# A hybrid mixer and top-4-of-32 expert layer on one core: selection and ranks inside the loop over token tiles, the row list built by one-hot matmuls

## What is computed

```python
x = layer_norm(ALPHA * x + g1 * y, ln1_g, ln1_b)
h = modulate(x, sh2, sc2)                      # the experts' input
logits = h @ w_router + b_router               # 1024 x 32
top_v, top_i = lax.top_k(logits, 4)
top_w = softmax(top_v)
# the 4096 (token, expert) pairs are sorted by expert; for each pair:
gate = minimum(h[tok] @ w_gate[e] + b_gate[e], 7)
up   = clip(h[tok] @ w_up[e] + b_up[e], -7, 7)
act  = (up + 1) * gate * sigmoid(1.702 * gate)
y[tok] += top_w * (act @ w_down[e] + b_down[e])
x = layer_norm(ALPHA * x + g2 * y, ln2_g, ln2_b)
```

## Time and profile before

| | us |
|---|---|
| median of 3 runs | 2768.78 |
| lowest, highest | 2767.74, 2773.34 |
| span of the profiled execution | 2767.4 |
| TensorE busy | 2457.2 (89%) |
| VectorE busy | 781.4 (28%) |
| ScalarE busy | 547.5 (20%) |
| GpSimd busy | 243.0 (9%) |
| data moved | 567.42 MB, mean 205 GB/s |

### The profile page before, as it was taken

One profiled execution on the slowest core, in us unless ns is written; L12 is line 12 of the kernel. 1 busy time (PEld: TensorE's weight loads), 2 busy tenths in 40 slices (PEclk: granted clock), 3 DMA queues, 4 the chain that ended last, 5 costly groups with the idle time before them and its releaser, 6 DMA issues.

```text
span 2767.4 us, 29927 instructions
## 1 busy us (share of the span) xinstructions
PE 2457.2 (89%) x8449; PEld 1158.9 (42%) x8450; DVE 781.4 (28%) x1123; ACT 547.5 (20%) x640; POOL 243.0 (9%) x274
## 2 busy tenths in 40 slices
PE   6899999678852899999999999999999999999992
PEld 2444444544441444444444344444443444444430
DVE  2443342743340122122222222212212222222225
ACT  2333343511100111111111111111112111112110
POOL 0000000002214000000000100000000000000000
PEclk9999999788855999999999999999999999999996
DMA  7212311112106476889749989846899647897634
GB/s 274 69 49 59 99 38 46 62 33 88 56 24 223 144 256 224 291 275 344 262 159 394 372 322 393 284 151 216 295 349 357 234 161 250 274 348 262 231 87 146
DMA packets 202656, 567.42 MB, mean 205 GB/s; under 512 B 17841, under 2 KB 67429, under 8 KB 202490
## 3 DMA queue, kind: packets, MB, share of 16 engines
q1 hardware_dynamic: 187450, 524.33, 51.9%
q0 software_dynamic: 15168, 42.57, 6.6%
HBM read 537.37 MB, written 33.66 MB: 206 GB/s over the span
## 4 chain that ended last, share of the span: by engine, by line
PE 82%; issue 6%; DVE 6%; SPq 2%; DMA 2%; ACT 1%; POOL 1%; DVEq 0%; POOLq 0%; ACTq 0%
PE psall L556 31%; PE psall L585 16%; PE psall L704 9%; PE psall L571 7%; PE psall L808 4%; PE psall L599 4%; PE psall L607 3%; PE psall L698 3%; DMA arena<-h_rows,lruw 2%; PE psall L677 1%; PE psall L684 1%; DVE arena L1247 1%; PE psall L823 1%; DVE arena L1279 1%; SPq L418 1%
## 5 line engine op out<-in xcount | busy, mean ns | idle before, releaser
L556 PE MATMUL psall<-arena 128*128 128x512 f32 x1984 | 867.2, 598 | 25.8 <-issue 25.8
L556 PEld LDWEIGHTS psall<-arena 128*128 128x128 f32 x1984 | 378.2, 192 | 494.2 <-issue 494.2
L585 PE MATMUL psall<-arena 128*128 128x512 f32 x992 | 434.3, 596 | 4.0 <-issue 4.0
L1496 DVE TENSOR_TENSOR arena<-psall,arena 64x512 f32<-64x512 f32 (+1 forms) x67 | 62.8, 937 | 1070.8 <-PE psall L556 825.1
L571 PE MATMUL psall<-arena 128*64 128x512 f32 x1152 | 261.9, 614 | 26.8 <-issue 26.6
L585 PEld LDWEIGHTS psall<-arena 128*128 128x128 f32 x992 | 187.2, 191 | 228.8 <-issue 228.8
L704 PE MATMUL psall<-arena 128*128 128x512 f32 (+3 forms) x656 | 265.7, 562 | 6.4 <-DMA wa_sb<-in_gla_wa_dram 6.4
L1067 ACT COPY arena<-psall 128x1024 f32<-128x1024 f32 x48 | 48.6, 1012 | 1017.8 <-PE psall L607 1017.8
L704 PEld LDWEIGHTS psall<-arena 128*128 128x128 f32 (+1 forms) x656 | 120.3, 185 | 139.9 <-issue 135.4
L571 PEld LDWEIGHTS psall<-arena 128*64 128x64 f32 x1152 | 97.0, 141 | 179.9 <-issue 179.9
L607 PE MATMUL psall<-ident,arena 128*128 128x128 f32 x712 | 97.5, 279 | 74.6 <-DMA arena<-h_rows,lruw 69.3
(11 more groups left out here) (250 smaller groups left out, 1708.3 us busy)
## 6 DMA issues: line engine op xcount, KB each, us to landing
arena<-in_w_gate_dram SPq DMA_DIRECT2D x128, 1024.0 KB
arena<-in_w_up_dram SPq DMA_DIRECT2D x128, 1024.0 KB
arena<-in_w_down_dram SPq DMA_DIRECT2D x128, 1024.0 KB, 7.1
arena<-in_w_ada_dram SPq DMA_DIRECT2D x32, 512.0 KB, 5.1
arena<-in_b_gate_dram SPq DMA_DIRECT2D x32, 512.0 KB, 5.9
arena<-in_b_up_dram SPq DMA_DIRECT2D x32, 512.0 KB, 7.1
arena<-in_b_down_dram SPq DMA_DIRECT2D x32, 512.0 KB
arena<-in_w_ada_dram SPq DMA_DIRECT2D x4, 2048.0 KB, 15.3
```

Source lines behind the costliest of these rows:

```text
L556: mm = pe.matmul(ps[2 * g + s], xT[:, k, :], ring[q][:, k % 2, s * BANK:(s + 1) * BANK], start=(k == 0), stop=(k == KD - 1))
L585: mm = pe.matmul(ps[6 + s], aT[:, k, :], ring[GUP + k // 2][:, k % 2, s * BANK:(s + 1) * BANK], start=(k == 0), stop=(k == KD - 1))
L1496: mm = dve.tensor_tensor(gb[p0:p1, 0:n], psG[p0:p1, 0:n], ebias[p0:p1, 0, c0:c0 + n], ALU.add)
```

## The change

- *Selection per tile.* `select(T)` does for one tile what was done behind the loop for all. In VectorE's instruction order select(t - 2) stands at the head of iteration t, and select(6) and select(7) stand behind the loop. The logits of every tile now go to the same 32 columns of PSUM bank 6 (`lgt_read` protects them). A running sum Mc of Mx over the tiles is kept.
- *Ranks per tile.* `ranks(T)` is one matmul with the triangle on Mx[T] and one with ones on Mc[T - 1]. In TensorE's order ranks(T - 1) stands behind the logits of tile T; ranks(7) and the counts (one matmul on Mc[7]) stand behind the loop.
- *Expert 0.* Its count is raised to at least 1, so it always has a job and the first job is always its own. SP issues the eight loads of its w_gate and w_up in the last pass of the loop, behind `out_mm` and ahead of the last h2 store, without the table. Its first bias rows no longer wait for a value from the table either.
- *The list.* The place of a row is now job * 128 + slot (half jobs use slots 64 to 127). VectorE makes for each token and choice a one-hot row over the 128 slots (`slot_is`) and one over the 64 jobs, times the token's number + 1 and times its weight (`job_is`). 32 matmuls of 128 columns add up, in PSUM, the list with slots on partitions and jobs in columns. An empty place holds 0. The indirect writes, `list_dram` and its loads are gone. A second matmul brings slots 64 to 127 to both halves for the half jobs.
- *Order at the end.* VectorE makes the index column for the gathers first (`moe_clear` 1), then the table's steps, then the rest. GpSimd's first gather no longer reads the table or waits for the residual stores; TensorE transposes its rows before it waits for the table.
- *Smaller.* The table loses the column number (7 entries for 8); VectorE and GpSimd read the column u of the list instead. The half job's gate and up matmuls read columns 64 to 127 of xT.

The diff, cut to its core:

```diff
+            def gu_pieces(e, u):
+                for q in range(GUP):
+                    if u is not None:
+                        sp.wait_ge(gu_used, GUP * u + (q + 1))
+                    w_v = (w_gate, w_up)[q % 2][0].rearrange("e (q c p) n -> e q p c n", c=2, p=P)[:, q // 2]
+                    sp.dma_start(ring[q], w_v[ds(e, 1)].rearrange("a p c n -> p (a c) n")).then_inc(d_gu[q], 16)
+
             for t in range(NT + 1):
+                if t == NT:
+                    sp.wait_ge(out_mm, 2 * NT)
+                    gu_pieces(0, None)
...
-            e0 = sp.value_load(tab[0:1, NC + J_E:NC + J_E + 1], min_val=0, max_val=NE - 1)
             for b in range(2):
                 sp.wait_ge(x_stored[b], 8 * NT)
-            gu_pieces(e0, None)
-
-            sp.wait_ge(rt_written, 16 + 16 * TOPK * NT)
-            list_v = list_dram.rearrange("(p c) a -> p (c a)", p=HT)
-            sp.dma_start(row_f[0:HT], list_v[:, 0:2 * CHUNKS].bitcast(F32)).then_inc(d_rowslot, 16)
-            sp.dma_start(row_f[HT:P], list_v[:, 2:2 * CHUNKS + 2].bitcast(F32)).then_inc(d_rowslot, 16)
-            sp.dma_start(row_h[0:HT], list_v[:, 0:2 * CHUNKS].bitcast(F32)).then_inc(d_rowslot, 16)
-            sp.dma_start(row_h[HT:P], list_v[:, 0:2 * CHUNKS].bitcast(F32)).then_inc(d_rowslot, 16)
             sp.wait_ge(moe_clear, 1)
-            bias_rows(e0)
+            bias_rows(0)
...
+            def ranks(T):
+                pe.wait_ge(sel_ready, T + 1)
+                if T:
+                    pe.matmul(ps[7][:, T * NE:(T + 1) * NE], ones[:, :], Mc[:, T - 1, :], start=True, stop=False,
+                              skip_group_check=True)
+                pe.matmul(ps[7][:, T * NE:(T + 1) * NE], tri[:, :], Mx[:, T, :], start=(T == 0), stop=True,
+                          skip_group_check=True).then_inc(rank_mm, 1)
...
+                    if T >= 1:
+                        pe.wait_ge(lgt_read, T)
                     for k in range(KD):
-                        mm = pe.matmul(ps[6][:, T * NE:(T + 1) * NE], h2T[:, k, :], wrt[:, k, :],
+                        mm = pe.matmul(ps[6][:, 0:NE], h2T[:, k, :], wrt[:, k, :],
                                        start=(k == 0), stop=(k == KD - 1))
                     mm.then_inc(logit_mm, 1)
-
-            pe.wait_ge(sel_ready, 1)
+                    if T >= 1:
+                        ranks(T - 1)
+
+            ranks(NT - 1)
+            pe.matmul(ps[7][:, NT * NE:(NT + 1) * NE], ones[:, :], Mc[:, NT - 1, :], start=True, stop=True,
+                      skip_group_check=True).then_inc(rank_mm, 1)
+
             for T in range(NT):
-                for s in range(T):
-                    pe.matmul(ps[0][:, T * NE:(T + 1) * NE], ones[:, :], Mx[:, s, :], start=(s == 0), stop=False)
-                pe.matmul(ps[0][:, T * NE:(T + 1) * NE], tri[:, :], Mx[:, T, :], start=(T == 0), stop=True)
-            for T in range(NT):
-                mm = pe.matmul(ps[1][:, 0:NE], ones[:, :], Mx[:, T, :], start=(T == 0), stop=(T == NT - 1))
-            mm.then_inc(rank_mm, 1)
-
-            pe.wait_ge(dest_ready, 1)
-
-            pe.wait_ge(tab_ready, 16)
+                pe.wait_ge(list_in, T + 1)
+                for k in range(TOPK):
+                    mm = pe.matmul(ps[0][:, 0:2 * JOBS], slot_is[:, T, k, :],
+                                   job_is[:, T, k, :, :].rearrange("p j a -> p (j a)"),
+                                   start=(T == 0 and k == 0), stop=(T == NT - 1 and k == TOPK - 1))
+            mm.then_inc(list_mm, 1)
+            pe.wait_ge(list_ready, 1)
+            for h in range(2):
+                mm = pe.matmul(ps[1][HT * h:HT * h + HT, 0:2 * JOBS], ident[:, HT:P],
+                               rows2[:, 0, :, :].rearrange("p j a -> p (j a)"), start=True, stop=True,
+                               skip_group_check=True)
+            mm.then_inc(half_mm, 1)
+
             pe.wait_ge(xg_ready, 16)
             turn(pe, xg, KD).then_inc(x_swapped, 1)
+            pe.wait_ge(tab_ready, 16)
...
+            def select(T):
+                dve.wait_ge(logit_mm, T + 1)
+                dve.tensor_tensor(lgt[:, T], ps[6][:, 0:NE], brt, ALU.add).then_inc(lgt_read, 1)
+                dve.wait_ge(lgt_read, T + 1)
+                link(dve.max(mx8[:, T], lgt[:, T]))
+                link(dve.max_index(ix8[:, T], mx8[:, T], lgt[:, T]))
+                link(dve.tensor_copy(ixf[:, T], ix8[:, T]))
+                link(dve.tensor_tensor(OH[:, T], iot.unsqueeze(1).to_broadcast([P, TOPK, NE]),
+                                       ixf[:, T, 0:TOPK].unsqueeze(2).to_broadcast([P, TOPK, NE]), ALU.is_equal))
+                link(dve.tensor_reduce(Mx[:, T], OH[:, T].rearrange("p k e -> p e k"), AX_X, ALU.add))
+                if T:
+                    link(dve.tensor_tensor(Mc[:, T], Mc[:, T - 1], Mx[:, T], ALU.add))
+                else:
+                    link(dve.tensor_copy(Mc[:, 0], Mx[:, 0]))
+                dve.nop().then_inc(sel_ready, 1)
...
+                if t == 1:
+                    dve.wait_ge(iota_ready, 3)
+                    link(dve.tensor_copy(iot, ioti2))
+                    link(dve.tensor_copy(slots, iota_i))
+                    link(dve.tensor_copy(jobcol, iota_i[:, 0:JOBS]))
+                    link(dve.tensor_scalar(id1, tokid, 1.0, None, ALU.add))
                 if t >= 2:
                     dve.wait_ge(x1_ready, t - 1)
+                if t >= 2:
+                    select(t - 2)
...
+            select(NT - 2)
+            select(NT - 1)
+            dve.tensor_tensor(ev, mx8[:, :, 0:TOPK], mx8[:, :, 0:1].to_broadcast([P, NT, TOPK]), ALU.subtract).then_inc(top_exp_in, 1)
+            dve.wait_ge(h2_turned, 2 * NT)
             for b in range(2):
                 dve.wait_ge(h2_stored[b], 8 * NT)
...
+            link(dve.tensor_scalar(r(CNT)[:, 0:1], r(CNT)[:, 0:1], 1.0, None, ALU.max))
...
+            link(dve.tensor_tensor(tmpO, OH, Gx.unsqueeze(2).to_broadcast([P, NT, TOPK, NE]), ALU.mult))
+            link(dve.tensor_reduce(pos, tmpO, AX_X, ALU.add))
+            link(dve.tensor_copy(posi, pos))
+            link(dve.tensor_scalar(loi, posi, P - 1, None, ALU.bitwise_and))
+            link(dve.tensor_scalar(hii, posi, 7, None, ALU.logical_shift_right))
+            link(dve.tensor_copy(slotf, loi))
+            link(dve.tensor_copy(jobf, hii))
...
+            dve.wait_ge(x_scaled, NT)
+            for T in range(0, NT, 2):
+                Ts = slice(T, T + 2)
+                dve.tensor_tensor(slot_is[:, Ts], slots.unsqueeze(1).unsqueeze(1).to_broadcast([P, 2, TOPK, P]),
+                                  slotf[:, Ts].unsqueeze(3).to_broadcast([P, 2, TOPK, P]), ALU.is_equal)
+                link(dve.tensor_tensor(job_is[:, Ts, :, :, 1], jobcol.unsqueeze(1).unsqueeze(1).to_broadcast([P, 2, TOPK, JOBS]),
+                                       jobf[:, Ts].unsqueeze(3).to_broadcast([P, 2, TOPK, JOBS]), ALU.is_equal))
+                link(dve.tensor_tensor(job_is[:, Ts, :, :, 0], job_is[:, Ts, :, :, 1],
+                                       id1[:, Ts].unsqueeze(3).to_broadcast([P, 2, TOPK, JOBS]), ALU.mult))
+                link(dve.tensor_tensor(job_is[:, Ts, :, :, 1], job_is[:, Ts, :, :, 1],
+                                       topw[:, Ts].unsqueeze(3).to_broadcast([P, 2, TOPK, JOBS]), ALU.mult))
+                dve.nop().then_inc(list_in, 2)
...
+            dve.wait_ge(list_mm, 1)
+            dve.tensor_copy(rows2[:, 0], ps[0][:, 0:2 * JOBS].rearrange("p (j a) -> p j a", a=2)).then_inc(list_ready, 1)
+            dve.wait_ge(list_ready, 1)
+            link(dve.tensor_scalar(tok_g[:, 1:1 + JOBS].unsqueeze(2), rows2[:, 0, :, 0:1], -1.0, 0.0, ALU.add, ALU.max))
+            dve.nop().then_inc(moe_clear, 1)
...
+                if t == 0:
+                    pool.iota(tokid, pattern=[[P, NT], [0, TOPK]], base=0, channel_multiplier=1).then_inc(iota_ready, 1)
+                    pool.iota(ioti2, pattern=[[1, NE]], base=0, channel_multiplier=0).then_inc(iota_ready, 1)
+                    link(pool.iota(tok1, pattern=[[0, 1]], base=0, channel_multiplier=1))
+                    pool.iota(iota_i, pattern=[[1, P]], base=0, channel_multiplier=0).then_inc(iota_ready, 1)
...
-            pool.wait_ge(rt_written, 16)
-            pool.wait_ge(dest_ready, 1)
-            pool.wait_ge(pair_ready, 1)
-            for k in range(TOPK):
-                for T in range(NT):
-                    pool.indirect_dma_start(out=list_dram, out_offset=bass.IndirectOffsetOnAxis(ap=dest[:, k, T:T + 1], axis=0),
-                                            in_=pair[:, k, T, :].bitcast(I32), in_offset=None).then_inc(rt_written, 16)
...
+            pool.wait_ge(moe_clear, 1)
+            gather(slice(1, 2), 1)
+            pool.wait_ge(moe_clear, 2)
             pool.wait_ge(tab_ready, 16)
-            pool.wait_ge(moe_clear, 1)
             for b in range(2):
                 pool.wait_ge(x_stored[b], 8 * NT)
```

(2 more changed lines are left out.)

205 lines of the change are left out of this document (82 added, 123 removed).

## The result

The changed kernel takes 2725.28 us (median of 4 runs, 2722.66 to 2731.07) against 2768.26 us (median of 4) for the kernel before on the same chip. The ratio is 0.9845 with a 95% interval of 0.9824 to 0.9866: 43 us faster, where 49.5 were forecast. A second set of five runs gave 2725.68 against 2772.06, ratio 0.9836 [0.9822, 0.9849], 46 us.

What follows compares the result with a forecast made beforehand. TensorE bounds the expert jobs; before them lies a hole. First matmul 832.7 + 3.9 + 0.5 = 837.1 against 884.58, -47.5; with -2 in the jobs -49.5, median 2719.3 us, range 2710 to 2730.

Steps and rivals of the forecast that it cites:

- Parts 1 and 2: Selects, ranks in tile loop: only select(7) on path, casts under 1 us each beside outproject(1), counts at 792.5 for 816.6.
- Part 2: Rank matmuls in TensorE's tile loop, behind the logits: nine before the last outprojection add 3.9 us.
- Part 3: Weights' load moved forward gains nothing alone; the last h2 store lands behind it, making VectorE 2.5 us later than the counts.
- Rival C: DMA ring order does not hold and the table is quick: -2.5 - 1, giving 2716 us; chance 0.13.
- B: The h2 store lands much later and holds VectorE, loads running at 248 GB/s: +13, 2732 us; chance 0.08.
- Parts 4 and 5: VectorE's rank arithmetic, 7.8 us, then its one-hot lists, 13.7 us, with TensorE's matmuls following; index column at 819.5.
- Rival A: TensorE's clock stays low under the one-hot matmuls: list ends at 822.7, +3.8, 2723 us; chance 0.17.
- Part 6: From list to first expert matmul: table later than gather, +8.0 plus 5.2 of control code, +13.2 us; matmul at 832.7.
- Part 7: Expert jobs: one column number less read per job, ahead of the gathers, -2 us, bounds 0 and -2.6.
- Rival E: Hole is set by another wait (bias rows, w_down), so the change misses its aim: 2719 + a few; chance 0.04.
- Rival D: Half jobs' gathers slow from reading token 0's row 64 times: 2809 us at 5 us each; chance 0.03.
- Part 8: select(6) beside POOL's h2 of tile 7 contends for SBUF, delaying the last logits: 0.5 us, bounds 0 and 1.9.

Runs made afterwards that it cites:

- the experiment: On the changed kernel, the eight loads of expert 0's w_gate and w_up issued behind the last h2 and residual stores: 2718.64 us (one run).
- the two combined versions: On the changed kernel, ranks in the wait and h2 store first, with the table's first steps early (2713.64 us) or casts early (2710.34 us).

## Why the prediction was right, and where it was not

- *Parts 1 and 2, the hole's side.* Right: one select on the path, and the counts 14.8 us behind the last X1 for 14.5. Hiding seven selects is worth 10.8 us net, 13 were forecast; 3.3 of what they take is covered by the rank matmuls beside them.
- *Part 2, the loop's side.* **Mis-sized.** 9 x 0.43 = 3.9 counts the instructions; the term measured 5.5 to 5.7 with the late rise of the clock. With the early rise, the case of the trace that the forecast was made from, ranks and selects together measured 3.7, and the casts of part 1, priced at nothing, 3.3. Right was where they stand, "behind the logits, and what is queued behind them is the next outprojection", and that TensorE's wait lies in front: moved there, they cost the loop nothing. The forecast's sign, a period 0.9 us longer from tile 3 on, did not come: the periods grow by 0.2 to 2.1 us, unevenly.
- *The base of the loop.* **The step that failed without being written:** I took 180.2 us of one trace as the loop's length. Its second trace has 183.1. So 2.9 of the 8.6 us between the two profiles shown are not the change. The forecast had +-2 for the shape of the median and nothing for this.
- *Part 3, the store.* Right in kind and size: landing 11.5 us, VectorE held; 2.5 forecast, 1.9 by the trace (805.72 to 807.60), 1.7 of the table's way and 1.2 of the hole by the experiment. "Alone gains nothing" is right too: with the weights behind the table the hole is shorter. Rival C, by which the ring order would not hold, is refuted, and so is B (+13).
- *Parts 4 and 5.* 7.8 forecast, 7.76 measured (807.60 to 815.36); the one-hot rounds 13.7 forecast, 13.6 measured (815.36 to 828.95). Rival A is refuted: the first 32 records take 5.94 us where VectorE needs 6.9 for two rounds, and the later rounds 2.05 per 16, the high level of the earlier trace rows. The clock does start at 0.50 under the first of them (818.75 to 820.00) and is 0.63 over the 5.94 us. The mean of the hole, 0.59, says little: TensorE is busy for 21.7 of its 54.6 us.
- *Part 6.* The table is the later of the two paths, as forecast: in ten traces the first matmul comes 5.62 to 5.66 us behind SP's first issue after the table, while from the transposes' start it varies between 7.0 and 8.4. Control code 5.65 for 5.2; the table's way 8.1 for 8.0. The changed kernel's [5.92 <-issue] is this control code.
- *Part 7, jobs.* **Wrong, small:** -2 forecast. Waits for gathers fell from 7.0 us to

```profile
PE psall L606 <- DMA arena<-h_rows,lruw: 6.0, 3, 2.8
```

  but the second trace of before has 5.6, and the others lie between 5.6 and 7.2: no fall is shown. The jobs' length scatters by more (1877.7 to 1886.9, but for the one above), with the time at the low clock. Rival E has nothing for it, the hole being what was forecast. Rival D is refuted: the gathers of half jobs, with 64 times the same row, let no wait grow (2.8 us at most, for 2.7).
- *Part 8, the shared port.* Not as argued. I priced GpSimd being held by VectorE, and beside VectorE's work its second step takes 2.48 us for 2.34, 0.1. It is VectorE that is held: the 32-column tensor_tensor of a select beside GpSimd's h2 takes 1.81 us where 0.19 is its time (select(6) at 794.12 and select(7) at 803.93 in the changed kernel; those in the loop take 1.80 to 1.81 too). A select in the loop therefore takes 3.8 us of VectorE, not 1.9 (88.55 us busy in the loop with the six, 65.91 without), and still lies in idle time: VectorE waits for the outprojection. "Under 1 us each" for the casts is wrong as well, two take 2.3 us; with the late rise they cost 0.0 (the two combined versions) and 0.3, with the early one 3.3.
- *Slips in the working.* Part 3's 792.5 + 1.3 + 1.4 is 795.2, not 795.0, and part 6's 1.4 + 4.1 + 2.0 is 7.5, not 7.6; neither moves the result. The 1.7 us of start-up in part 3 is in no row; the eight loads took 22.8 us from the first issue to the last landing, for 22.3.
- *The sum.* Hole -52.0 (-51.4 forecast, with the port); loop +5.7 in the late case of the clock, +6.8 in the early one (+3.9); jobs 0 (-2). That gives -46 and -45 where the medians show -43 and -46. The misses, 1.8 to 2.9 us in the loop and 2 in the jobs, all go one way and are small beside the hole, which was read right.

## What to carry to other kernels

A chain that is taken off the end of a loop must be put where each engine waits, not only where it has time in sum: the rank matmuls cost 5.5 us behind the logits and nothing in the wait just before them. Before a term of a few us is read from the difference of two traces, take a second trace of the unchanged kernel; here the same program had loops of 180.2 and 183.1. And a prefetch is worth only what someone waits for: 8 MB loaded 55 us early gained nothing, and held a 0.5 MB store ahead of the critical chain.

## What the runs showed of the hardware that I had not expected

- **TensorE's clock at the start of a burst.** After 11.9 to 13.4 us of idling, the granted clock rose from 1.2 to 2.4 GHz 2.8 to 3.0 us into the first outprojection in four of the fourteen traces, and 4.9 to 6.2 us into it in ten. For the kernel before the difference is 1.5 us in the first tile and 2.9 in the loop, since the clock also rises elsewhere in each later tile; for the changed kernel it is 1.8 (187.0 for 188.8).
- **VectorE waits for GpSimd, for the whole instruction.** Casts of 32 and 64 columns took 2.32 and 2.22 us and a two-input tensor_tensor of 32 columns 1.81, each until 0.04 or 0.05 us behind the end of GpSimd's tensor_tensor; GpSimd itself lost 0.1. The Trainium skill, "SBUF — State Buffer", section "Who interferes with whom", says that a VectorE instruction with two SBUF inputs contends with a GpSimd instruction that reads SBUF, that a cast can contend too, in a 2-port mode, and that whoever issues first gets the shared ports for the whole instruction. The trace agrees, down to GpSimd's instruction being the earlier one at each of the three.
- **The jobs' length follows the clock.** With 86 us at the low level the jobs took 1871.0 us, with 119 us 1886.9 (the second trace of before); the length less half the time at the low level is 1827 to 1830 us in all fourteen traces.
- **A small store is seen late behind a gather:** 3.2 and 3.0 us instead of 1.4, on another queue than the gather's.
